# The first layer's MLP in the seven-product form, with the next layer's modulation summed in small portions

## The reference

```python
for l in range(2):
    mod = silu(cond) @ mod_w[l] + mod_b[l]      # 1024 -> 6 * 1024, for c and for c_ctx
    sh1, sc1, g1, sh2, sc2, g2 = split(mod, 6)
    h = rmsnorm(x, norm_mix[l]) * (1 + sc1) + sh1
    x = x + g1 * mixer(h)
    h = rmsnorm(x, norm_mlp[l]) * (1 + sc2) + sh2
    a = relu(h @ mlp_w1[l])                     # 1024 -> 4096
    x = x + g2 * ((a * a) @ mlp_w2[l])          # 4096 -> 1024
y = rmsnorm(x, final_norm)
```

## Time and profile before

| | |
|---|---|
| median of 3 runs | 2579.92 us (2578.02 to 2585.79) |
| the profiled execution, its own time | 2586.16 us |
| its span | 2584.0 us |
| MLP of layer 0 (plain) | about 580 to 1404 us of the span |
| MLP of layer 1 (seven products) | about 1790 to 2558 us of the span |

### The profile page before, as it was taken

One profiled execution on the slowest core, in us unless ns is written; L12 is line 12 of the kernel. 1 busy time (PEld: TensorE's weight loads), 2 busy tenths in 40 slices (PEclk: granted clock), 3 DMA queues, 4 the chain that ended last, 5 costly groups with the idle time before them and its releaser, 6 DMA issues.

```text
span 2584.0 us, 42044 instructions
## 1 busy us (share of the span) xinstructions
PE 2526.6 (98%) x15122; PEld 2469.9 (96%) x15122; DVE 1784.2 (69%) x3188; ACT 796.5 (31%) x1266; POOL 756.5 (29%) x561
## 2 busy tenths in 40 slices
PE   7999999999999999999999999999999999999998
PEld 6999999999999999999999888889999999999997
DVE  5878878658575585675769888956756556656674
ACT  5333322222011011020115666723423422432323
POOL 1221212322222222222222000122445445545531
PEclk9999999999999999999999999999999999999999
DMA  6422222312222222222222211132111111111131
GB/s 252 155 74 69 87 70 75 123 53 70 66 74 73 65 81 65 73 73 65 73 73 71 105 41 41 29 142 80 41 49 49 32 49 49 33 48 49 41 123 74
DMA packets 261656, 190.72 MB, mean 74 GB/s; under 512 B 9285, under 2 KB 253765, under 8 KB 260294
## 3 DMA queue, kind: packets, MB, share of 16 engines
q1 hardware_dynamic: 260004, 174.71, 22.2%
q10 hardware_dynamic: 1570, 14.93, 1.4%
HBM read 170.20 MB, written 19.41 MB: 73 GB/s over the span
## 4 chain that ended last, share of the span: by engine, by line
PE 85%; DVE 11%; issue 2%; ACT 1%; DMA 0%; SPq 0%; POOL 0%; DVEq 0%; ACTq 0%; POOLq 0%
PE psum L828 68%; PE psum L1159 12%; DVE mod_sum L1777 2%; PE psum L1209 2%; PE psum L855 1%; DVE h_lo L1810 1%; DVE h_lo L1803 1%; DVE sumsq L1748 1%; DVE x L1834 1%; DVE sumsq L1819 1%; DVE mod_sum L1772 1%; DVE s_bwd L2190 0%; DVE xc L2300 0%; PE psum L1024 0%; PE psum L1015 0%
## 5 line engine op out<-in xcount | busy, mean ns | idle before, releaser
L828 PE MATMUL psum<-h_hi,w_hi 128*128 128x384 f32 (+1 forms) x2880 | 673.5, 342 | 12.3 <-POOL w_lo L700 5.2
L828 PE MATMUL psum<-h_lo,w_hi 128*128 128x384 f32 (+1 forms) x2880 | 659.1, 337 | 0.0
L828 PE MATMUL psum<-h_hi,w_lo 128*128 128x384 f32 (+1 forms) x2880 | 658.8, 337 | 0.0
L828 PEld LDWEIGHTS psum<-h_hi,w_hi 128*128 128x128 f32 x2880 | 514.0, 189 | 27.0 <-issue 14.0
L828 PEld LDWEIGHTS psum<-h_lo,w_hi 128*128 128x128 f32 x2880 | 518.3, 189 | 0.0
L828 PEld LDWEIGHTS psum<-h_hi,w_lo 128*128 128x128 f32 x2880 | 517.3, 189 | 0.0
L698 POOL CAST w_hi<-w_raw 128x1024 fp32r<-128x1024 f32 x106 | 112.8, 1064 | 1127.9 <-PE psum L828 682.5
L1777 DVE SCALAR_TENSOR_TENSOR mod_sum<-mod_raw,cond,mod_sum 128x128 f32<-128x128 f32 x1120 | 333.6, 367 | 10.2 <-DVE mod_sum L1777 2.0
L1834 DVE SCALAR_TENSOR_TENSOR x<-psum,mod,x 128x768 f32<-128x768 f32 (+2 forms) x264 | 145.8, 610 | 236.7 <-PE psum L828 236.7
L1993 DVE TENSOR_TENSOR x<-x,psum 128x576 f32<-128x576 f32 x280 | 203.6, 752 | 104.4 <-PE psum L1159 104.1
L700 POOL TENSOR_TENSOR w_lo<-w_raw,w_hi 128x1024 fp32r<-128x1024 f32 x106 | 257.3, 2427 | 8.5
(11 more groups left out here) (302 smaller groups left out, 3091.4 us busy)
## 6 DMA issues: line engine op xcount, KB each, us to landing
w_raw<-in_mlp_w SPq DMA_DIRECT2D x128, 512.0 KB, 4.1
mod_raw<-in_mod_w SPq DMA_DIRECT2D x160, 256.0 KB, 2.9
w_raw<-in_ab_w_in SPq DMA_DIRECT2D x24, 512.0 KB, 4.4
x_spill<-x ACTq DMA_DIRECT2D x2, 4608.0 KB, 13.7
w_raw<-in_lru_w_in SPq DMA_DIRECT2D x16, 512.0 KB, 4.4
x<-x_spill SPq DMA_DIRECT2D x2, 2880.0 KB, 9.5
x_old<-x_spill SPq DMA_DIRECT2D x8, 576.0 KB, 6.6
x_rows<-in_x_sample SPq DMA_DIRECT2D x8, 512.0 KB, 6.8
```

The source lines that it names most:

```text
L828: mm = pe.matmul(psum[:, s, c, 0:end - c * CH], w, v[:, k, c * CH:end], start=(first and n == 0 and w is hi[k] and v is in_hi), stop=(last ...
```

## The change

1. `SPLIT_MLP` is (0, 1): layer 0 uses `split_mlp` too. `mlp` is gone, and semaphore counts are shifted by what layer 0 has counted (`past`). Layer 0 gets the spill of `x`, its clearing and its loading back.
2. The modulation of layer 1 is made in 24 pairs of columns: an instruction covers 256 elements, 16 for a pair. Three pairs are summed in `out_proj(0)` (8 instructions after each of the tiles 1 to 6), and 3 in each of the seven groups: 36 instructions between the stages of the hidden tiles and 4 in the reads of each of the first three weight units (`pair_ops`).
3. The weights of the modulation come in quarters of a pair (256 KB, rows of 1 KB in place of 512 B) into two buffers; quarter m is issued when the steps of quarter m-2 are done. The quarters stand between the weight loads in SP's order.
4. PE adds a pair over the partitions with four one-column matmuls (`pair_columns`).
5. The squares of odd hidden tiles lie in `b_sum` in place of a tile of their own, to make room.
6. The scratch for dynamic DMAs is 1024 in place of 4096.

```diff
-SPLIT_MLP = (1,)
+SPLIT_MLP = (0, 1)
+WIDE_MODS = 2
+OUT_PAIRS = GRP_PAIRS = 3
+PAIR_BUFFER = (0, 1, 0)
+PAIR_STEPS = 2 * KT
+QUARTER = PAIR_STEPS // 4
...
+            def load_quarter(g, m):
+                sp.wait_ge(pair_step, at(g, GRP_PAIRS * PAIR_STEPS, STEP0 + QUARTER * (m - 1)))
+                ...
+                sp.dma_start(pair_raw[:, m % 2], w.rearrange("(k p) m -> p k m", p=P)).then_inc(pair_landed[m % 2], 16)
...
+                    if l == 0 and c > 1:
+                        load_quarter(None, 2 * (c - 2))
+                        load_quarter(None, 2 * (c - 2) + 1)
...
+                    first(g, 1)
+                    first(g, 2)
+                    quarters_of(0, 1)
+                    first(g, 3)
+                    quarters_of(2, 3)
+                    first(g, 4)
+                    quarters_of(4, 5)
+                    second(g, 0, c)
+                    quarters_of(6, 7)
+                    second(g, 1, c + 1)
+                    quarters_of(8, 9)
+                    second(g, 2, c + 2)
+                    quarters_of(10)
+                    second(g, 3, c + 3)
+                    quarters_of(11)
...
+            def pair_columns(g, n, batch):
+                pe.wait_ge(pair_step, at(g, GRP_PAIRS * PAIR_STEPS, STEP0 + PAIR_STEPS * (n + 1)))
+                ...
+                        last = pe.matmul(dst, pair_sum[:, PAIR_BUFFER[n % GRP_PAIRS], c, e * P:(e + 1) * P], ones[:, 0:1], start=True, stop=True)
...
+            def pair_ops(g, pairs, first, end):
+                for i in range(pairs * PAIR_STEPS + first, pairs * PAIR_STEPS + end):
+                    ...
+                    if k == 0:
+                        dve.tensor_scalar(total, w, s, None, ALU.mult).then_inc(pair_step, 1)
+                    else:
+                        dve.wait_ge(pair_step, at(g, GRP_PAIRS * PAIR_STEPS, STEP0 + i - 1))
+                        dve.scalar_tensor_tensor(out=total, in0=w, scalar=s, in1=total, op0=ALU.mult, op1=ALU.add).then_inc(pair_step, 1)
...
+                    if l == 0 and k:
+                        pair_ops(None, 0, 8 * (k - 1), 8 * k)
...
+                        if step and j in (3, 5):
+                            pair_ops(g, OUT_PAIRS, step + j - 3, step + j - 1)
...
                     even(g, 0)
-                    blocks_done(g, 0)
+                    pairs(0, 12)
                     scale(g, 1)
+                    pairs(12, 16)
                     odd(g, 1)
+                    pairs(16, 24)
                     blocks_done(g, 6)
                     scale(g, 2)
+                    pairs(24, 28)
                     even(g, 2)
+                    pairs(28, 32)
                     scale(g, 3)
+                    pairs(32, 36)
                     odd(g, 3)
...
-            mlp(0)
+            split_mlp(0)
...
-    nc = bacc.Bacc("TRN2", target_bir_lowering=False, num_devices=1, dynamic_dma_scratch_size=4096)
+    nc = bacc.Bacc("TRN2", target_bir_lowering=False, num_devices=1, dynamic_dma_scratch_size=1024)
```

More of the change, by code:

```diff
@@ L585, in split_mlp, with quarters_of @@
                 with sp.Fori(0, SEVEN_GROUPS) as g:
[L586 to L589, removed]
+                    def quarters_of(*which):
+                        if l == 0:
+                            for m in which:
+                                load_quarter(g, 4 * OUT_PAIRS + m)
+                    c = U + GRP + 1
+                    first(g, 1)
[13 more added lines that the diff above has]
+                    quarters_of(11)
                 g = SEVEN_GROUPS
@@ L717, in _ @@
             split(outs, 1)
[L718 to L736, removed]
+            with pool.Fori(outs + 1, AT_MLP[0].units // 2) as i:
                 split(i, 0)
@@ L1079, in out_proj @@
                     project(None, 0, I + c, 0, U + c, width=TOK, free=out_passed if c == KT - 1 else None).then_inc(unit_done, 1)
[L1081 to L1117, removed]
-                                pe.wait_ge(split_done, at(g, GRP_UNITS, unit + 3))
-                            second(unit, half, range(GRP)).then_inc(unit_done if half else mini_done, 1)
-                        if j > 1:
-                            mod_col(2 + j)
-                group(0)
-                with pe.Fori(1, GROUPS) as g:
-                    group(g)
@@ new lines, in out_proj @@
+                    if l == 0 and c in (4, 6):
+                        pair_columns(None, c // 2 - 2, 0)
+            def pair_columns(g, n, batch):
+                pe.wait_ge(pair_step, at(g, GRP_PAIRS * PAIR_STEPS, STEP0 + PAIR_STEPS * (n + 1)))
+                pe.wait_ge(mod_read, at(g, 1, FIRST_BATCHES + HEADS + batch))
+                start = at(g, 4 * GRP_PAIRS, 2 * (MODS + WIDE_MODS * n))
+                for e in range(WIDE_MODS):
+                    for c in range(2):
+                        column = start + 2 * e + c
+                        dst = mod_psum[:, column:column + 1] if isinstance(column, int) else mod_psum[:, ds(column, 1)]
+                        last = pe.matmul(dst, pair_sum[:, PAIR_BUFFER[n % GRP_PAIRS], c, e * P:(e + 1) * P], ones[:, 0:1], start=True, stop=True)
+                last.then_inc(mod_used, WIDE_MODS)
@@ L1936, in split_mlp, with scale @@
                 norm = 2 * l + 2
-                def scale(g, j):
+                def scale(g, j, plain=False):
                     s = (I + j) % 2
@@ L2045, in split_mlp @@
                 with_old(1)
[L2046 to L2047 removed]
+                scale(g, 2, True)
                 with_old(2)
```

278 lines of the change are left out of this document (129 added, 149 removed).

## The result

| | before | after |
|---|---|---|
| median of the runs on the same chip | 2580.57 us (2578.02 to 2585.79) | 2560.39 us (2559.11 to 2561.81) |
| ratio | | 0.9913 [0.99, 0.9927] |
| span of the profiled execution | 2584.0 us | 2557.3 us |

By the ratio the change is worth 22.4 us (18.8 to 25.8 by its interval); the two medians of the table differ by 20.2. I had forecast 2550 us, with a range of 2540 to 2570. The spans differ by 26.7 us, but 3.0 of these lie ahead of everything that the change touches. PE has one wait for GpSimd in the output projection that every version shows alike, 0.70 us, at 499.00 before and at 496.02 after. In the eleven profiles of this study it stands between 490.8 and 499.0, though nothing ahead of it was edited. So I measure from this mark to the end of the span: 2085.0 us before, 2061.3 after, **23.7 less**. The forecast for this was 29.9.

The account below looks back on a forecast made before the run. PE, busy 98% of the span, was taken as the bound: 38.3 us less work minus 8.4 us of entry waits gives 29.9 us, from the median 2579.92 to 2550 us, range 2540 to 2570.

Parts of the forecast that it names:

- PE's gain, 38.3: Layer 0's MLP: PE's work falls from 823.9 to 785.6 us, with 24 pairs of columns at 0.80 us each included.
- Steady groups at nothing: Layer 0's steady groups: the modulation sums fit DVE's spare time and cost PE nothing; groups of 97.5 us.
- R1: Rival: sums in the products' reads delay PE 1 us in each of 21 units, 2571 us; chance 0.18 together with R3.
- R2: Rival: in the products' reads sums cost 1.89 us each beside POOL, 78 us in all, 2628 us; chance 0.07.
- Entry, 8.4: Entry into layer 0's MLP: PE's waits and a clock drop, five terms, sum to 8.4 us.
- (a): Squares at the entry: the output projection's last 8 sums go ahead of DVE's chain to them, +2.0 us.
- (b): Hidden tile 3 at the entry: 12 sums and a late weight quarter delay its scale(1), +1.1 us.
- (c): Hidden tile 4 at the entry: sums delay scale(2), POOL's split falling on other work; +2.0 us, bounds 0.2 to 3.8.
- R3: Rival: weights come late through SP's order, 3 us in each of seven groups, 2571 us; chance 0.18 together with R1.
- (d): First product at the entry: its second half waits for block T3 from DVE, +2.0 us, from 1.2 up to 3.
- (e): Entry: PE's granted clock may drop to 0.97 after its wait, costing under 3.7 us; +1.3 us taken.
- R4: Rival: the entry costs next to nothing and layer 0's tail gains a little, 2543 us; chance 0.10.

Follow-up runs that it names:

- e4: Kernel after, with the modulation sums of all seven layer-0 groups left out (counts still made, modulation wrong): 2554.49 us, ratio 0.9897 to before.
- e1: Kernel after, with the 48 modulation sums of layer 0's first seven-product group left out (counts still made): 2547.71 us, ratio 0.9869 to before.
- e10: e5 with the 4 sums before odd(3) moved out, so all four weight units have 4 sums in their reads: 2554.03 us, ratio 0.9887 to before.
- e6: Kernel after, with x cleared by GpSimd and the first group's 48 sums left out: 2549.18 us, ratio 0.9863 to before.
- e2: Kernel after, with the 8 sums after tile 6 of the output projection done after tiles 1 to 5: 2556.59 us, ratio 0.9905 to before.
- e5: Kernel after, with the edits of e2 and e3 together, whole computation: 2549.0 us, ratio 0.9864 to before.
- e9: Kernel after, with the 36 sums between hidden-tile stages in two blocks, 24 and 12, SP's order unchanged: 2577.99 us, ratio 0.9978 to before.
- e3: Kernel after, with x cleared by GpSimd instead of DVE in both layers, nothing left out: 2552.43 us, ratio 0.988 to before.
- e8: Kernel after, with 32 of the 36 sums between hidden-tile stages in one block before tile 1's reading: 2571.65 us, ratio 0.9952 to before.

## Why the prediction was right, and what was off

The mechanism held: PE's work fell, the steady groups hid all that DVE took on, and the entry cost some of it. Against the 6.2 us that are missing:

- **PE's gain, 38.3.** A pair of columns takes (97.75 - 95.09) / 3 = 0.887 us, not 0.80. 24 of them: 2.1 us less gain. The refilling behind them was the term that I had guessed.
- **Steady groups at nothing.** Right: 97.75 us for 97.5 forecast, no wait, and with the portions of all seven groups left out (e4) the groups are as long, and the mark is within 0.1 us of where it is without the first group's alone (e1). R1 and R2 don't happen. e10 shows why the bound by POOL's longest instruction did not apply in the reads: there it lies in the fourth unit, which has no sums. Between the stages of the hidden tiles it is met, and DVE's idle time covers it.
- **Entry, 8.4.** The mark to the second group took 204.5 us. With e6's entry (103.85), the stretch of before (87.05) and two pairs of columns (1.77) it would take 192.7, so the entry costs **11.8 us**, 3.4 more than the sum. By its terms:
  (a) 1.7 where I had 2.0 (90.54 - 87.05 - 1.77). The size is right and the way is not: the portion took 6.20 and not 3.3, and the wait for the squares did not grow (2.41 us, 2.35 before); a second wait of 1.36 for a low part came ahead of it. e2 gets 2.5 us back.
  (b) 0.93 where I had 1.1.
  (c) 3.16 where I had 2.0, within 0.2 to 3.8. I had hoped that POOL's split would fall on other work. It fell on `odd(1)` again, with 3.75 us for two sums of blocks and 5.00 for four low parts (1.55 and 3.36 undisturbed), so of my two bounds the upper one was the nearer. The split had waited 10.53 us for a DMA behind the quarters, which is the sign that I had named for R3; but in e1, where it did not, the same work took 4.42 and 5.43, so the late weights are not what put it there. No wait of PE is shown to come from them.
  (d) 1.99 where I had 2.0, but right by chance: the product that waited was the third, for the reading of tile 4, and not the first, for T3. I had worked out when T3 is due and never when that reading is.
  (e) 3.1 where I had 1.3. This is the term that failed most: I allowed for a part of one slow stretch, behind the wait for the squares. There the clock stayed at 1.00, and there were two, of 1.6 and 1.5, behind the waits at tile 4 and at the third product.
  These make 10.9; the last 0.9 was not resolved.
- **The rest**, 0.7 us, is a difference of two. From the squares of layer 0's MLP to the next squares the traces have 828.45 us before and 799.34 after, 29.1 less, and the output projection takes 3.5 more: 4.3 short of the forecast, where the terms above make 5.5. The rows are those of TensorE, before (its first squares stand at 586.05, those of the kernel after at 586.56), then after:

```profile
1414.50 0.91 PE L877 MATMUL psum<-sumsq,ones 128*128 128x384 f32 x2 [0.59 <-DVE sumsq L1748]
```

```profile
1385.90 0.91 PE L928 MATMUL psum<-sumsq,ones 128*128 128x384 f32 x2 [1.03 <-DVE sumsq L1752]
```

Behind these next squares, where both kernels do the same work, the kernel after takes 1.9 us more, 0.7 in layer 1's mixer and 1.2 behind its MLP; the nine others show this too (0.6 to 1.9, and 0.9 to 1.4). Neither the 1.2 too few nor the 1.9 has a cause that a run shows. The median lies 10.4 us above the forecast, 4 more than the profile behind the mark explains; the interval of the ratio is 7 us wide, and the part ahead of the mark moves by 8 us between the profiles.

R4 (an entry for next to nothing) was wrong for this version; e5 comes near to it, at 2549.0.

**The best version** is e5, the whole computation with two edits of order: 2549.0 us, 0.9864 [0.9848, 0.9881] of before, where the change alone has 0.9913 [0.99, 0.9927].

## What to carry to other kernels

Added work on an engine with room to spare is paid where a stage starts, since there that engine has no lead yet; move what can be moved off it there (here the clearing, 7.3 us), before touching the steady loop. Spare time in a loop is worth only what each due time leaves: the same sums cost a steady group nothing in small portions, 1.2 to 3.8 us in blocks, and 1.1 when four of them stand in the last reads before the next group, beside GpSimd's long instruction. Check each reading that a product waits for, not only the one that looks latest.

## What the runs showed of the hardware

- A wait of PE of 1.9 to 3.2 us is in some cases followed by some 3 us of matmuls at 1.2 GHz and in others not, at the same place of the same program: behind waits of 1.94 to 2.01 us in e9 four times of six, behind the one of 1.99 in the kernel after and 2.00 in e2, but not in e3 (1.99), e5 (2.00) or e10 (1.98). Behind the wait for layer 0's squares, 1.4 to 2.5 us, it came in e8 and e9 and in none of the nine others. Such a stretch cost 1.4 to 1.6 us, a half to four fifths of the wait ahead of it. What decides it these runs don't tell. Behind e8's waits of 1.3 to 1.4 us there was none.
- GpSimd clears 128 x 9216 elements about as fast as VectorE (timeline of GpSimd in e5; VectorE took 7.74 us):

```profile
593.33 7.80 POOL L791 MEMSET x<- 128x9216 f32 x1
```

- What DVE's instructions lose beside GpSimd's depends on how many of them meet: the same four low parts took 3.36 us with GpSimd idle (e6), 4.89 beside two of its low parts (e6) and 6.52 beside four (e5). One sum of 0.42 us took 2.60 beside a GpSimd instruction of 2.45 (e10).
